# Moving the 128-token expert pair from first to third place in a routed feed-forward stage

## The reference, cut to what matters

```python
def swiglu(h, w1, w3, w2):
    return (jax.nn.silu(h @ w1) * (h @ w3)) @ w2

def moe_swiglu(h, router, w1, w3, w2):
    t = h.reshape(B * S, D)
    vals, idx = lax.top_k((t @ router).astype(jnp.float32), TOP_K)
    wts = jax.nn.softmax(vals, axis=-1)
    comb = jnp.sum(jax.nn.one_hot(idx, N_EXPERTS) * wts[..., None], axis=1)
    for e in range(N_EXPERTS):
        out = out + comb[:, e:e + 1] * swiglu(t, w1[e], w3[e], w2[e])
```

## Time and profile before

| what | before |
|---|---|
| median of three runs | 2698.48 us |
| lowest and highest run | 2696.84 and 2698.78 us |
| span of the profiled execution | 2698.3 us |
| PE busy | 2619.8 us, 97% of the span |
| DVE busy | 1267.2 us, 47% |
| ACT busy | 515.9 us, 19% |
| bytes moved | 707.17 MB, mean 262 GB/s |
| routed stage, first gather to last release of its ring | 760.7 to 1628.8 us |

### The profile page before, as it was taken

How to read it: one execution, slowest core, us unless ns; L and a number is a source line. 1 busy time by engine, 2 the same in 40 slices (tenths; PEclk the granted TensorE clock), 3 DMA queues, 4 the chain that set the end, 5 groups by cost and what they waited for, 6 DMA issues and landing times. The chain is left out here.

```text
span 2698.3 us, 53707 instructions
## 1 busy us (share of the span) xinstructions
PE 2619.8 (97%) x23522; PEld 2084.3 (77%) x23522; DVE 1267.2 (47%) x2634; ACT 515.9 (19%) x1020; POOL 93.8 (3%) x181
## 2 busy tenths in 40 slices
PE   7999999999979999899899999999999999999999
PEld 6788999978955546646646648788999997889998
DVE  2555797475621101101101104676589736765883
ACT  3322100333210000000000003243122123331220
POOL 0000011000100000000000000000000000000000
PEclk9999999999979999999999999999999999999999
DMA  9536686655479998999999995335654553444432
GB/s 375 189 151 232 240 285 232 238 203 180 164 290 401 417 392 367 425 427 411 426 426 408 425 424 209 133 139 187 224 209 182 211 220 127 148 174 186 170 135 102
DMA packets 70360, 707.17 MB, mean 262 GB/s; under 512 B 7792, under 2 KB 8048, under 8 KB 31600
## 3 DMA queue, kind: packets, MB, share of 16 engines
q1 hardware_dynamic: 44640, 610.92, 56.4%
q0 software_dynamic: 25488, 92.81, 9.8%
HBM read 702.65 MB, written 1.05 MB: 261 GB/s over the span
## 5 line engine op out<-in xcount | busy, mean ns | idle before, releaser
L1109 PE MATMUL psum<-hT,ring 128*128 128x256 f32 x2816 | 621.5, 380 | 0.0
L1109 PEld LDWEIGHTS psum<-hT,ring 128*128 128x128 f32 x2816 | 531.6, 190 | 76.8 <-ACT work L1728 2.0
L1390 PE MATMUL psum<-ring,work 128*32 128x256 f32 x6720 | 372.1, 382 | 24.3 <-DMA ring<-in_m 22.7
L1390 PEld LDWEIGHTS psum<-ring,work 128*32 128x32 f32 x6720 | 236.6, 111 | 157.4 <-issue 30.9
L2447 DVE TENSOR_TENSOR work<-work,psum 128x256 f32<-128x256 f32 (+1 forms) x84 | 32.6, 388 | 480.8 <-ACT work L1754 480.8
L1109 PE MATMUL psum<-work,ring 128*128 128x256 f32 x1096 | 239.5, 379 | 0.3 <-DVE work L1924 0.3
L1109 PEld LDWEIGHTS psum<-work,ring 128*128 128x128 f32 x1096 | 207.5, 190 | 29.4 <-ACT work L1728 0.7
L2490 DVE CUSTOM_DVE_ANT_0 mod_in<-mod_in,c_rows,cols 128x1024 f32<-128x1024 f32 x152 | 192.4, 1278 | 27.2 <-DMA mod_in<-in_mods 27.0
L1149 PE MATMUL psum<-work,ring 128*128 128x128 f32 x1392 | 175.6, 275 | 0.0
L2637 POOL DMA_DIRECT2D mod_in<-in_mods x176 | 93.1, 529 | 2339.3 <-DVE ada L2490 2293.7
L1124 PE MATMUL psum<-hT,ring 128*128 128x128 f32 x1408 | 164.4, 279 | 3.0 <-DVE hT L2104 1.9
(11 more groups left out here) (282 smaller groups left out, 2783.8 us busy)
## 6 DMA issues: line engine op xcount, KB each, us to landing
ring<-in_m SPq DMA_DIRECT2D x112, 2048.0 KB, 16.9
work<-in_m SPq DMA_DIRECT2D x56, 2048.0 KB, 17.4
ring<-in_w_in SPq DMA_DIRECT2D x46, 2048.0 KB, 8.7
mod_in<-in_mods POOLq DMA_DIRECT2D x176, 512.0 KB, 5.7
ring<-in_up SPq DMA_DIRECT2D x22, 2048.0 KB, 8.4
ring<-in_f SPq DMA_DIRECT2D x11, 2048.0 KB, 8.9
ring<-in_down SPq DMA_DIRECT2D x16, 1408.0 KB, 6.7
ring<-in_w_o SPq DMA_DIRECT2D x8, 2048.0 KB, 9.1
```

Source lines behind the costliest of these rows:

```text
L1109: last = mm(gbank(it["bank"])[:, j, :], wt[:, k, col0 + j * P:col0 + (j + 1) * P], rhs[:, k0 + k, :], start=(n == 0), stop=(n == total - 1))
L1390: last = mm(o[32 * j:32 * j + 32, at * T:(at + 1) * T], picked[n][:, k, 32 * part:32 * part + 32], wts[j // 2][:, k, j % 2 * T:(j % 2 + 1) ...
```

## The change

The 128-token slot becomes slot 4, the wide expert of pair 2. Slots 0, 2 and 6 hold 96 tokens. The rank that goes to each wide slot is 1, 2, 0, 3, so the fullest expert still gets the 128 tokens. The narrow slots are as before. Every test of the pair number that stood for "the wide one" becomes a test for `LARGE`. The number of loads, their sizes and the depth of the ring stay.

```diff
+LARGE = 2
+WIDE_RANK = (1, 2, 0, 3)
...
-    put("rank", (np.arange(8) // 2 + 4 * (np.arange(8) % 2)).astype(np.float32)[None, :])
-    put("width", np.where(np.arange(8) % 2, 64.0, np.where(np.arange(8), 96.0, 128.0)).astype(np.float32)[None, :])
+    put("rank", np.where(np.arange(8) % 2, np.arange(8) // 2 + 4, np.repeat(WIDE_RANK, 2)).astype(np.float32)[None, :])
+    put("width", np.where(np.arange(8) % 2, 64.0, np.where(np.arange(8) // 2 == LARGE, 128.0, 96.0)).astype(np.float32)[None, :])
...
-        steps += [("w", s, (0, 1)), ("w", s, (2,) if q else (2, 3)), ("n", s, (0, 1))]
+        steps += [("w", s, (0, 1)), ("w", s, (2, 3) if q == LARGE else (2,)), ("n", s, (0, 1))]
...
-    return (32, 96) if q else (0, 128)
+    return (0, 128) if q == LARGE else (32, 96)
...
-        for part in range(3 if q else 2):
+        for part in range(2 if q == LARGE else 3):
...
-                    if q == 0:
+                    if q == LARGE:
                         for half in range(2):
                             last = mm(outs[half], hid_e[0][:, f, :], wt[:, half * 512:(half + 1) * 512],
...
-                rows = 96 if q else P
+                rows = P if q == LARGE else 96
...
-                    if q:
+                    if q != LARGE:
                         A(y_e[0][32 * part:32 * part + 32, 3 * T:4 * T], o[96:128, 0:T], ACT.Copy).then_inc(
...
-                    out = hid_e[1] if kind == "n" else hid_e[0] if q == 0 else hid_wide
+                    out = hid_e[1] if kind == "n" else hid_e[0] if q == LARGE else hid_wide
```

More of the change, by code:

```diff
@@ L1396, in down @@
             def down(r, q):
-                banks = [bank_at[q, "down_w", part] for part in range(3 if q else 2)]
+                banks = [bank_at[q, "down_w", part] for part in range(2 if q == LARGE else 3)]
                 outs = [bank_of(r, b) for b in banks]
                 def wide(f, wt):
-                    if q == 0:
+                    if q == LARGE:
                         for half in range(2):
```

## The result

The changed kernel takes 2702.47 us (median of 12 runs, 2700.95 to 2705.26), the kernel before 2698.95 us in the runs made beside it. The medians differ by 3.5 us. The ratio, estimated from the single runs, is 1.0017 with a 95% interval from 1.0009 to 1.0024, which is 4.6 us (2.4 to 6.5). The change makes the kernel slower, clear of no change by the interval, and the ratio lies inside the 0.2% that the forecast called no change, though the interval's upper end lies just over it. The forecast was 3.3 us.

What follows compares the result with a forecast made beforehand. PE was taken to bound the 128-token pair, loads the 96-token pairs. Four pair lengths, 216.3 + 211.2 + 231.4 + 198.8 = 857.7 us against 854.4, added 3.3 us to 2698.48: 2701.8 us, range 2697.8 to 2706.0.

Steps and rivals of the forecast that it cites:

- What bounds which pair: Routed stage: the 128-token pair goes at PE's pace, 96-token pairs at the loads' pace, 426 GB/s.
- Pair 0: First pair, now 96 tokens: its end set by arrival of chunks, 216.3 us, 18.1 us less than before.
- Pair 1: Second pair, unchanged but with the wider gather at its end, 0.85 us more: 211.2 us.
- Pair 2: Third pair, now 128 tokens: never waits for weights, old first pair's 234.4 us less 3.0 of half clock, 231.4 us.
- Pair 3: Last pair, starting from a full ring with a stop of some 14 us: 198.8 us.
- The other engines: ACT, DVE, SP and POOL in the routed stage: their work moves with the pair, adding nothing to the sum.
- The stop behind the wide pair: Boundary after the 128-token pair: full ring halts loads some 14 us, named as cost beside 18 to 20 us surplus.
- The sum: All four pairs of the routed stage: 857.7 us, 3.3 us more than the 854.4 before.
- A: Third pair's surplus absorbed by its neighbours' slack: 17.7 us less, 2680.8 us; chance 0.05.
- B: Third pair starves for loads as well, adding waits of 7.6 us: 2709.4 us; chance 0.10.
- C: Half clock at the start of the third pair, 3.0 us: 2704.8 us; chance 0.04.
- D: Ranks and widths no longer match, so a second pass is needed, about 854 us more; chance 0.01.

Runs made afterwards that it cites:

- all_96: The changed kernel with no 128-token pair, the fullest expert's tokens beyond 96 left out; ratio to the kernel before 0.993.
- two_128: The changed kernel with pairs 0 and 2 both computing 128 tokens; ratio to the kernel before 1.0077.
- large_second: The changed kernel with the 128-token pair in second place (pair 1); ratio to the kernel before 1.0012.
- large_last: The changed kernel with the 128-token pair in last place (pair 3); ratio to the kernel before 1.0013.
- gather_twice: The changed kernel with every gather behind the first issued twice into the same banks; ratio to the kernel before 1.0058.
- warm_first: The kernel before with eleven useless matmuls between the first gather and first weights, to keep PE's clock up; 2696.7 us, ratio 0.9985.
- late_first: The kernel before with each pair's scatter moved behind the first group of the next pair; ratio 0.9987.
- ring5_third: The changed kernel with five buffers in the ring in place of six; one run, 2741.0 us.
- warm_third: The changed kernel with eleven useless matmuls between the first gather and first weights; ratio to the kernel before 1.0007.

## Why the prediction was right

Point by point, by its own steps:

- **What bounds which pair.** Held: 426 GB/s in pairs 0 and 1, 414 in pair 2 with PE busy all through; `all_96` and `two_128` show that it is the width and not the place.
- **Pair 0**, 216.3 forecast (215.4 to 217.3), measured 215.4 here and 215.3 to 215.8 in `all_96`, `large_second` and `large_last`. It is the largest miss of the sum, 0.9 us, and two errors stand behind it. The arrival needed at pair 1's start was put at 46.3 to 46.7 chunks; the changed kernel's own window, first row below, has 419 GB/s over 230.5 us, which is 96.6 MB or 46.1 chunks, some 2 us less than the middle. And the 0.8 us for the earlier first release were taken off although the sum already had 426 GB/s from 792 on. The dip that they stand for is real (second row, before, 246 GB/s; third row, after, 410), but it lies behind 792, so it was counted twice. The two errors go opposite ways; that they cancel in part is luck.

```profile
760.00:990.50 230.50, 209.70 (x3128) 134.06 (x3129) 24.04 (x68) 14.18 (x44) 0.00 (x0) 0.96 0.99 419
```

```profile
792.00:794.00 2.00, 2.00 (x44) 1.17 (x40) 0.61 (x2) 0.00 (x0) 0.00 (x0) 1.00 0.94 246
```

```profile
792.00:794.00 2.00, 1.86 (x36) 0.82 (x28) 0.00 (x0) 0.00 (x0) 0.00 (x0) 1.00 0.98 410
```

- **Pair 1**, 211.2 forecast, 211.1 measured. The 0.85 us of the wide gather measure 0.86, and `gather_twice` shows that such time is paid in full there.
- **Pair 2**, 231.4 forecast, 231.6 measured, and 231.6 in second place as well. It had no half clock, and `warm_first` reached 231.6 in pair 0 by taking the half clock away there, which closes that term from the other side. The term was put at 3.0 us and measures 2.8 in the execution that the sum used. The lower bound of 230.9 has no row behind it.
- **Pair 3**, 198.8 forecast, 198.9 measured.
- **The other engines** at nothing: in pair 0, now short of chunks, PE waits 2.6 us for DVE (1.5 and 1.1), as it did in pair 1 before; the loads set that pair's end. In pair 2 PE waits for no engine.
- **The stop behind the wide pair.** The prediction's short form, "its 18 to 20 us of surplus plus the full-ring stop wherever it stands ahead of another pair", counts one thing twice, though its sum does not. `large_last` has no stop and costs as much: 220.6 against 199.3 us for a narrow last pair, 21.3 us, where the third place adds 20.3 (231.6 against 211.3). The stop is the same surplus seen from the loads.
- **The sum**: +3.3 forecast, +2.6 in the lengths, +3.8 in the spans. The rest of the span's difference is ahead of the stage (0.7) and behind it (0.5), in code that the change doesn't touch. The start of the first weights lay between 771.9 and 775.4 us in the executions profiled, so a single span can't carry a difference of 1 to 3 us. Nor is a sum of lengths that sharp: with the low clock of `late_first` in place of its own, before's sum would be 853.3 and the difference 3.7. The medians of 12 runs give 3.5, the ratio 2.4 to 6.5. The forecast agrees with all of these; that it meets the medians to 0.2 us is luck.

Of the rivals, A was refuted by two runs. B did not occur, and its price was misread: the 22.7 us of the earlier trace rows hold the 5.0 us ahead of pair 0's weights, so a third of the rest is 5.9 and not 7.6. `ring5_third` shows B one buffer away, at 12.7 us: the margin that the prediction worked out from rates (405 against 413 GB/s, six chunks that last 31 us) was right for six buffers and would not have been for five. C did not occur, and D did not either: the stage has one pass in both.

The Trainium skill, in "TensorE: Matmul & The Clock Gate", section "HAM oscillation", describes a loop whose compute per tile is shorter than its wait. The prediction saw the starved pair 0 at risk by it, but that condition is not met here: a group of `up` is 17.5 us of PE work, and PE's waits within pair 0 are 3.0 us at most. In the trace pair 0 has a mean clock of 0.98, so the half clock does not come at every group. Its length would hardly change in any case, as `warm_third` shows for its start.

## What to carry to other kernels

When a loop is fed through a ring of fixed depth, work out for each item whether the compute or the loads are slower, and add up the item lengths; moving the heavy item does not spread its surplus over neighbours that wait, because idle time is not stored and only a ring's depth is handed on. An order can still change small costs. A slow clock at the start lengthens an item that the compute sets (2.8 us here) and hardly one that the loads set (at most 0.4). Extra compute at a boundary counts in full in both, once the ring fills before its first release; only ahead of the very first item, where PE waits for a load anyway, was it free. Before moving work that frees no buffer to another place, count how many buffers are free there, since the stop may only be cut in two.

## What was unexpected of the hardware

With five buffers of 2 MB in place of six, both the loads and PE lost time in the same pair: 388 GB/s, and PE idle 10 of 200 us, where each alone could do better (426 GB/s, and a pair of 231.6 us). One buffer was worth 40 us of 857 in the changed kernel and 33 us of 854 in the one before.

The low clock behind the idle gap lasted differently long for nearly the same gap. The first weights took 18.7 us for 320 records in the changed kernel after 5.6 us of idle PE and 20.1 us in `all_96` after 6.0 us, where 17.5 us is the time at full clock. Nothing in these runs says what sets it. It matters for the method: a single profile of the kernel before can be 1 us off in this one term.
